# Second attention of a fused transformer kernel: rotary queries from a reordered weight, keys of two heads in one product, squares of the feed-forward residual on ScalarE

## The chip, the cores and the metric

The kernel runs on one core of a Trainium2 chip. One launch computes two transformer blocks for a single sequence of 256 tokens of width 1024, all in 32-bit floats. The metric is the device time of a launch in microseconds (us); the result is compared with the time of the kernel before, measured on the same chip.

## The reference, cut to what matters

The change touches the second half of the first block: the latent attention with shared keys and values (16 heads, handled as 8 pairs), and the norm that follows each of the two feed-forward layers.

```python
def rmsnorm(x, g):
    inv = lax.rsqrt(jnp.mean(x * x, axis=-1, keepdims=True) + RMS_EPS)
    return (x * inv) * g

def rope(x, positions):                  # x: ... x 32
    ang = positions[..., None] * inv_freq    # 16 frequencies
    cos, sin = jnp.cos(ang), jnp.sin(ang)
    x1, x2 = x[..., :16], x[..., 16:]
    return jnp.concatenate([x1 * cos - x2 * sin, x1 * sin + x2 * cos], axis=-1)

def mla_shared_kv(h, ...):
    a = rmsnorm(h, kv_norm) @ w_kv_a                 # 256 + 32 columns
    c_kv = rmsnorm(a[..., :256], ckv_norm)
    k_rope = rope(a[..., 256:][:, :, None, :], positions)   # one for all heads
    k_nope = jnp.einsum('bsr,rhd->bshd', c_kv, w_uk)        # 16 heads x 64
    v = jnp.einsum('bsr,rhd->bshd', c_kv, w_uv)
    return jnp.concatenate([k_nope, broadcast(k_rope)], -1), v

def mla_attention(xn, positions, k, v, ...):
    c_q = rmsnorm(xn @ w_dq, cq_norm)                # 768 wide
    q = (c_q @ w_uq).reshape(B, S, 16, 64 + 32)
    q = jnp.concatenate([q[..., :64], rope(q[..., 64:], positions)], -1)
    o = causal_block_attention(q, k, v, 1 / sqrt(96))
    return o @ w_o

h = h + mla_attention(rmsnorm(h, attn_norm), ...)
h = h + swiglu(rmsnorm(h, ffn_norm), w_gate, w_up, w_down)   # ends both layers
```

## The kernel before, in words

The program is written by hand, engine by engine, in one block for each: `sp` (SyncE) starts the loads, `pe` (TensorE) multiplies, `act` (ScalarE) and `dve` (VectorE) empty PSUM and do the elementwise work. Nothing is reordered by a scheduler: the order of the work on an engine is the order in which its function is written. Engines meet at semaphores. For each of the eight PSUM banks there is `full` (a product is ready) and `free` (it has been read); `take(b)` and `evacuated(b)` on TensorE wait until bank b has been read. Weights come through four buffers `SLOT0` to `SLOT3`: `fill(s, ...)` on SyncE waits until slot s is used up, `here[s]` says that its load has landed, and `release(s)` gives it back when the next product that is passed to `first` completes. Each slot is a single buffer: the next load of a slot starts only after its last product.

Around the change the work runs like this.

1. The first feed-forward layer (`ffn(0)`) ends with its four output tiles (128 tokens x 512 columns each) in banks 0 to 3. `residual` on VectorE adds each to H and squares the sum, with a running sum for the norm. TensorE waits for this.
2. A norm for two users follows. `turned` multiplies H by a diagonal matrix (L533), which scales and turns it in one step, into banks 0 to 3. `gained` (L1769, L1770) reads each bank twice on VectorE, once with the gain of the key norm (into XT2) and once with that of the attention norm (into XT). Ahead of this VectorE clears WPAD, a weight of 96 columns, in which only 64 to 95 are filled (the 32 rope columns of `w_kv_a`, by a load that ScalarE issues). With it the rope part of the keys comes out on partitions 64 to 95.
3. Tables of cosine and sine, the latent keys and queries, and the values follow.
4. Then come the eight head pairs. `mla_proj` computes a pair's queries (12 products, 96 weight columns for each head), then its keys (4 products, 64 columns for each head), and then multiplies the copied queries QRAW by the matrix `rot` (L866, L867), which swaps and negates the rope halves. `rotate` on VectorE makes q x cos + rot(q) x sin in three operations (L2026, L2027, L2029) into QT. `mla_scores` (L874, L875) waits for it. `attend` then turns the probabilities (`flip`, L508), multiplies them by the values (`mix_values`, L502) and turns the output of the pair before.

In the loop over the pairs TensorE does: scores of pair i, projection of pair i+1, attention of pair i. So a projection lies between the scores and the probabilities that come from them, and the pair's own scores come one turn later. Only for pair 0 do the scores follow its projection directly.

At the end of the second feed-forward layer the residual is the same as in the first. After it comes a norm by rows instead of item 2.

## Time and profile before

| | us |
|---|---|
| median of 3 runs | 1939.9 (1938.97 to 1947.72) |
| the profiled execution | 1941.62 |
| its span, first to last instruction | 1939.5 |
| TensorE busy | 1697.2 (88%) |
| VectorE busy | 1054.5 (54%) |
| ScalarE busy | 515.4 (27%) |

The times in the rows are microseconds from the start of the span, then the duration, except where a row says ns. L502 is line 502 of the kernel. Many lines are those of helpers: L502 is every grouped product. A product of 32-bit floats shows as two matmul records, so that 16 products are "x32". PE is TensorE, PEld its weight loads, DVE VectorE, ACT ScalarE, SPq SyncE's queue, ps a PSUM bank. Consecutive matmul records overlap, so the durations of single records don't add up; the times in the chain of waits do. The attention pairs of the change run from 433.8 to about 556 us of the span.

### The profile page before, as it was taken

The numbers are of one execution on the slowest core, as the hardware profiler recorded it, in microseconds if no ns is written. First come the engines' busy times: TensorE is split into PE (matmuls) and PEld (weight loads), VectorE is DVE, ScalarE is ACT, GpSimd is POOL, SyncE is SP. The second block draws the span as 40 slices with busy tenths as digits, with TensorE's granted clock in tenths as the row PEclk, the third lists the DMA queues.
The fourth block names the chain that finished last, engine by engine and source line by source line (L and its number), as shares of the span: only waits on it lengthen the run. The fifth ranks groups of instructions, "written<-read, shape, count | busy, mean of one in ns | idle before, by whom it ended". The sixth has DMA issues, their size and how long they took to land.

```text
span 1939.5 us, 22425 instructions
## 1 busy us (share of the span) xinstructions
PE 1697.2 (88%) x7681; PEld 1178.4 (61%) x7681; DVE 1054.5 (54%) x2463; ACT 515.4 (27%) x1029; POOL 345.8 (18%) x296
## 2 busy tenths in 40 slices
PE   6798999889989998999899999778788878888876
PEld 5787999756649997786565468443333434344332
DVE  5464555533445555255535311477766677766764
ACT  2353444213334442232310001121222222222211
POOL 2550000000000000000000000145344344444440
PEclk9899999999999999999999999989899989889989
DMA  7342665402436654143302415099999999999995
GB/s 240 109 109 88 195 183 177 146 15 60 137 92 184 190 179 140 44 152 131 145 30 88 151 56 196 31 420 420 421 421 421 422 420 421 421 420 422 421 421 240
DMA packets 209719, 435.38 MB, mean 224 GB/s; under 512 B 11649, under 2 KB 145153, under 8 KB 175745
## 3 DMA queue, kind: packets, MB, share of 16 engines
q0 software_dynamic: 36864, 268.45, 33.3%
q1 hardware_dynamic: 171760, 166.06, 27.0%
q8 instruction: 36, 0.59, 0.1%
q10 hardware_dynamic: 1040, 0.13, 0.0%
q14 instruction: 19, 0.15, 0.0%
HBM read 433.53 MB, written 1.05 MB: 224 GB/s over the span
## 4 chain that ended last, share of the span: by engine, by line
PE 68%; DMA 18%; DVE 9%; issue 3%; ACT 1%; POOL 1%; SPq 0%; DVEq 0%; POOLq 0%; ACTq 0%
PE ps L502 37%; DMA OT<-in_peer_uv,IX 16%; PE ps L1297 11%; PE ps L688 6%; PE ps L1002 3%; PE ps L1015 3%; PE ps L533 1%; DMA SLOT<-in_fox_w_in 1%; PE ps L508 1%; DVE SLOT L2422 1%; PE ps L592 1%; DVE SLOT_R L1823 1%; PE ps L1094 1%; PE ps L1212 1%; DVE AR L2137 1%
## 5 line engine op out<-in xcount | busy, mean ns | idle before, releaser
L1706 POOL DMA_INDIRECT SLOT<-in_peer_uv,IX x128 | 134.6, 1052 | 1370.5 <-DVE IX L2416 1123.0
L1297 PE MATMUL ps<-SLOT,AR 128*128 128x512 f32 x512 | 264.6, 673 | 102.5 <-ACT AR L1636 102.5
L1297 PEld LDWEIGHTS ps<-SLOT,AR 128*128 128x128 f32 x512 | 108.5, 217 | 252.2 <-issue 129.6
L502 PE MATMUL ps<-ARH 128*128 128x256 f32 x2112 | 257.0, 283 | 5.2 <-DVE SM L1854 5.2
L502 PEld LDWEIGHTS ps<-ARH 128*128 128x128 f32 x2112 | 256.2, 192 | 7.0 <-issue 5.5
L2422 DVE SCALAR_TENSOR_TENSOR SLOT<-SLOT,V 128x1024 f32<-128x1024 f32 x128 | 153.4, 1225 | 78.9 <-DMA SLOT<-in_peer_uv,IX 76.9
L1823 DVE TENSOR_TENSOR ARH<-SLOT,ARH 128x2048 fp32r<-128x2048 f32 (+1 forms) x88 | 154.1, 1756 | 47.8 <-ACT ARH L1375 31.1
L1297 PE MATMUL ps<-AR 128*128 128x512 f32 x320 | 142.8, 594 | 11.4 <-ACT AR L1636 11.4
L502 PE MATMUL ps<-XT,SLOT 128*128 128x256 f32 x576 | 126.6, 380 | 1.3 <-DVE XT L1770 1.3
L688 PE MATMUL ps<-ARH 128*128 128x512 f32 x528 | 123.9, 390 | 0.0
L502 PEld LDWEIGHTS ps<-XT,SLOT 128*128 128x128 f32 x576 | 108.9, 190 | 16.9 <-issue 1.9
L502 PE MATMUL ps<-SLOT,XT 128*128 128x512 f32 (+3 forms) x320 | 114.6, 517 | 4.0 <-DVE XT L1770 2.6
L1630 ACT ACTIVATE AR<-AR 128x4 f32<-128x4 f32 x64 | 13.1, 205 | 382.7 <-DVE SLOT L2422 182.2
L1297 PEld LDWEIGHTS ps<-AR 128*128 128x128 f32 x320 | 59.7, 190 | 84.0 <-issue 64.3
L688 PEld LDWEIGHTS ps<-ARH 128*128 128x128 f32 x528 | 97.7, 188 | 19.4
L2422 DVE SCALAR_TENSOR_TENSOR AR<-AR,V 128x1024 f32<-128x1024 f32 x80 | 95.3, 1222 | 24.4 <-DMA AR<-in_peer_uv,IX 24.3
L1706 POOL DMA_INDIRECT AR<-in_peer_uv,IX x80 | 90.7, 1134 | 77.2 <-PE ps L1297 72.0
L502 PEld LDWEIGHTS ps<-SLOT,XT 128*128 128x128 f32 x320 | 58.0, 190 | 57.8 <-issue 48.7
L1837 DVE TENSOR_TENSOR AR<-AR,ps 128x256 f32<-128x256 f32 x44 | 18.5, 421 | 125.4 <-ACT AR L1385 125.4
L1636 ACT ACTIVATE AR<-CT,AR 128x128 f32<-128x128 f32 x256 | 81.8, 390 | 17.5 <-DVE AR L2436 17.5
L1375 ACT CAST ARH<-SLOT 128x2048 fp32r<-128x2048 f32 x44 | 83.3, 1897 | 0.0
L502 PE MATMUL ps<-XT 128*128 128x256 f32 (+1 forms) x288 | 60.9, 367 | 7.9 <-DMA XT<-in_w_pq_by_head 5.8
(378 smaller groups left out, 2437.9 us busy)
## 6 DMA issues: line engine op xcount, KB each, us to landing
SLOT<-in_w_gate SPq DMA_DIRECT2D x44, 512.0 KB, 4.0
SLOT<-in_w_up SPq DMA_DIRECT2D x44, 512.0 KB, 5.3
SLOT<-in_w_down SPq DMA_DIRECT2D x44, 512.0 KB, 5.6
SLOT<-in_w_in SPq DMA_DIRECT2D x9, 2048.0 KB, 8.6
SLOT<-in_fox_w_in SPq DMA_DIRECT2D x16, 512.0 KB, 5.3
XT<-in_w_pq_by_head SPq DMA_DIRECT2D x8, 1024.0 KB
SLOT<-in_mla_w_uq SPq DMA_DIRECT2D x8, 576.0 KB
SLOT<-in_fox_w_in SPq DMA_DIRECT2D x2, 2048.0 KB, 13.0
```

Source lines behind the costliest of these rows:

```text
L502: m = pe.matmul(outp, l, r, start=(n_ == 0), stop=(n_ == len(pairs) - 1))
L508: return pe.transpose(outp, src, IDENT)
L533: m = pe.matmul(ps[:, b, n_ * P:(n_ + 1) * P], src[:, n_ % 2, k * P:(k + 1) * P], DG[:, n_ % 2, :], start=True, stop=True)
L688: m = pe.matmul(ps[:, o_, :], l_, r_, start=(start and b == 0 and n_ == 0), stop=(stop and b == 1 and n_ == 2))
L1002: m = pe.matmul(ps[:, b, :], cols(XT, t, k), slot(s_, KC, 512)[:, k, :], start=(k == 0), stop=(k == KC - 1))
L1015: m = pe.matmul(ps[:, b, h * P:(h + 1) * P], l(h), r(h), start=True, stop=True)
L1297: m = pe.matmul(ps[:, 2 * t + c, :], DIAG[:, j, :], v_row(j)[:, c * 512:(c + 1) * 512], start=False, stop=False)
L1375: act.copy(WGU[:, b, 0].rearrange("p g k n -> p (g k n)"), SLOT[b][:, 0:2 * KC * P]).then_inc(sem("high_ready"), 1)
L1636: act.activation(DIAG[:, j, :], IDENT, ACT.Copy, scale=AV[:, t, j:j + 1]).then_inc(sem("diag_ready"), 1)
L1706: pool.indirect_dma_start(PAIR[j], None, pairs, bass.IndirectOffsetOnAxis(IX[:, t, j:j + 1], 0)).then_inc(gathered[j], 16)
L1823: return TT(out_, x, high.bitcast(F32), ALU.subtract)
L2422: m = STT(u_row(j), u_row(j), 1.0, V[:, t, :], ALU.mult, ALU.mult, accum_out=DOT[:, t, j:j + 1])
```

## The change

**Queries.** The host lays out the query weight by pairs in 256 columns instead of 192: for the first head its 64 plain columns, its 32 rope columns, and the same 32 with their halves swapped; for the second head the rope columns, the swapped ones, then the plain ones. The product itself now gives the swapped copy. One table TABQ holds 1 for the plain rows, cosine for the rope rows and signed sine for the swapped ones, and `rotate` is one product of the PSUM bank with it. The rotated keys stand on all 32-row groups, so that the scores' sum over 128 rows adds the cosine and the sine parts. The products with `rot` and the QRAW copy of each pair go; the load of each pair's query weight grows from 576 to 768 KB.

**Keys.** The keys of both heads of a pair are one group of 2 products with 128 columns instead of two groups of 2 with 64. ScalarE copies the result in two pieces of 64 partitions by 256 instead of one of 64 by 512.

**Key rope.** WPAD becomes a loaded weight of 128 columns (`w_krope`, the 32 columns four times, 512 KB) in the upper half of SLOT3. The clearing, the signal and ScalarE's load go. TensorE waits for `here[3]` twice 16 ahead of this product instead of ahead of the values.

**The norm for two users.** VectorE writes only XT2; ScalarE writes XT from the same banks after it. TensorE starts when XT2 is whole (`norm_low`), and waits for banks 2 and 3 later.

**Squares.** At the end of both feed-forward layers VectorE only adds and signals (`grown`), and ScalarE squares with a running sum; VectorE waits for `squared`.

```diff
-            fill(3, (slot(3, 2, D), w_uv))
-            qk(rows(w_uq, 0, 192), w_uk[:, :, 0:P])
+            fill(3, (WPAD, rows(a["w_krope"], 0, P)), (slot(3, 2, D), w_uv))
+            qk(rows(w_uq, 0, 2 * P), w_uk[:, :, 0:P])
             with T.loop("mla", PAIRS - 1) as i:
-                qk(dyn(w_uq, i * 192 + 192, 192), w_uk[:, :, ds(i * P + P, P)])
+                qk(dyn(w_uq, i * 2 * P + 2 * P, 2 * P), w_uk[:, :, ds(i * P + P, P)])
...
-            norm_t()
-            pe.wait_ge(sem("wpad_here"), T.next(sem("wpad_here"), 17))
+            turned(H, KC, freer="a")
+            pe.wait_ge(here[3], T.next(here[3], 32))
+            pe.wait_ge(sem("norm_low"), T.next(sem("norm_low"), 4))
             take(4)
-            group(ps[0:96, 4, 0:S], ((WPAD[:, k, :], XT2[:, k, :]) for k in range(KC))).then_inc(full["a"][4], 1)
+            group(ps[:, 4, 0:S], ((WPAD[:, k, :], XT2[:, k, :]) for k in range(KC))).then_inc(full["a"][4], 1)
             T.add(free["a"][4])
...
             pe.wait_ge(here[2], T.next(here[2], 16))
+            evacuated(2, 3)
...
-                    m = group(ps[0:96, 0, hh * S:(hh + 1) * S], ((slot(0, 6, 192)[:, k, 96 * hh:96 * hh + 96], CQT[:, k, :]) for k in range(6)))
+                    m = group(ps[:, 0, hh * S:(hh + 1) * S], ((slot(0, 6, 2 * P)[:, k, P * hh:P * hh + P], CQT[:, k, :]) for k in range(6)))
                 release(0)
-                m.then_inc(full["a"][0], 1)
-                T.add(free["a"][0])
+                m.then_inc(full["v"][0], 1)
+                T.add(free["v"][0])
                 pe.wait_ge(here[1], T.next(here[1], 16))
                 take(6)
-                for hh in range(2):
-                    m = group(ps[0:64, 6, hh * S:(hh + 1) * S], ((slot(1, 2, P)[:, k, 64 * hh:64 * hh + 64], CKT[:, k, :]) for k in range(2)))
+                group(ps[:, 6, 0:S], ((slot(1, 2, P)[:, k, :], CKT[:, k, :]) for k in range(2))).then_inc(full["a"][6], 1)
                 release(1)
-                m.then_inc(full["a"][6], 1)
                 T.add(free["a"][6])
-                take(7)
-                evacuated(0)
-                first(pe.matmul(ps[0:96, 7, 0:S], const("rot", 96), QRAW[0:96, 0, :], start=True, stop=True))
-                pe.matmul(ps[0:96, 7, S:2 * S], const("rot", 96), QRAW[0:96, 1, :], start=True, stop=True).then_inc(full["v"][7], 1)
-                T.add(free["v"][7])
 
             def mla_scores(i):
-                evacuated(6, 7)
+                evacuated(0, 6)
                 for hh in range(2):
...
+                for c in range(2):
+                    for t in range(NT):
+                        act.wait_ge(sem("grown"), T.next(sem("grown")))
+                        m = act.activation(XS[:, t, c * 512:(c + 1) * 512], H[:, t, c * 512:(c + 1) * 512], ACT.Square,
+                                           accum_out=SS[:, 10 + NT * c + t:11 + NT * c + t])
+                m.then_inc(sem("squared"), 1)
...
-            act.wait_ge(sem("wpad_here"), 1)
-            act.dma_start(WPAD[:, :, 64:96], rows(a["w_kv_a"], 256, 288)).then_inc(sem("wpad_here"), 16)
+            for g in range(4):
+                act.wait_ge(sem("norm_low"), T.next(sem("norm_low")))
+                for k in (2 * g, 2 * g + 1):
+                    m = act.activation(XT[:, k, :], ps[:, g, k % 2 * S:k % 2 * S + S], ACT.Copy, scale=gcol("attn1", k, 1))
+                m.then_inc(free["a"][g], 1)
             act.wait_ge(sem("angle_ready"), T.next(sem("angle_ready")))
-            act.activation(COS[0:96, 0, :], ANG[0:96, 0, :], ACT.Sin)
-            act.activation(SIN[0:96, 0, :], ANG[0:96, 1, :], ACT.Sin).then_inc(sem("sin_ready"), 1)
+            act.activation(COS, ANG[:, 0, :], ACT.Sin)
...
             def mla_copy():
-                act.wait_ge(full["a"][0], T.next(full["a"][0]))
-                act.copy(QRAW[0:96, :, :], view(ps[0:96, 0, :], 2, S)).then_inc(free["a"][0], 1)
                 act.wait_ge(full["a"][6], T.next(full["a"][6]))
-                act.copy(KT[0:64, :, :], view(ps[0:64, 6, :], 2, S)).then_inc(free["a"][6], 1)
+                act.copy(KT[0:64, 0, :], ps[0:64, 6, 0:S])
+                act.copy(KT[64:P, 1, :], ps[64:P, 6, 0:S]).then_inc(free["a"][6], 1)
 
...
+            def ffn_residual():
+
+                for c in range(2):
+                    for t in range(NT):
+                        b = 2 * t + c
+                        dve.wait_ge(full["v"][b], T.next(full["v"][b]))
+                        half = H[:, t, c * 512:(c + 1) * 512]
+                        TT(half, half, ps[:, b, :], ALU.add).then_inc(free["v"][b], 1)
+                        T.add(free["v"][b])
+                        settled(b)
+                        signal("grown")
+                dve.wait_ge(sem("squared"), T.next(sem("squared")))
...
-            dve.memset(WPAD[:], 0.0).then_inc(chain, 1)
+            scaled(H, D, squared=True).then_inc(sem("xs_ready"), 1)
+            for g in range(4):
+                dve.wait_ge(full["v"][g], T.next(full["v"][g]))
+                TT(XT2[:, 2 * g:2 * g + 2, :], view(ps[:, g, :], 2, S), inner(gcol("kv", 2 * g, 2), S), ALU.mult).then_inc(sem("norm_low"), 1)
...
-            signal("wpad_here")
-            norm("attn1", X2=XT2, name2="kv")
...
-            dve.tensor_copy(COS[R96, 1, :], COS[R96, 0, :])
-            dve.tensor_copy(SIN[R96, 1, :], SIN[R96, 0, :]).then_inc(chain, 1)
+            dve.memset(TABQ[0:64, 0, :], 1.0)
+            dve.memset(TABQ[64:P, 1, :], 1.0)
+            dve.tensor_copy(TABQ[64:96, 0, :], COS[64:96])
+            dve.tensor_copy(TABQ[0:32, 1, :], COS[0:32])
+            TS(TABQ[96:P, 0, :], SIN[96:P], const("sign")[96:P], None, ALU.mult)
+            TS(TABQ[32:64, 1, :], SIN[32:64], const("sign")[32:64], None, ALU.mult).then_inc(chain, 1)
...
-            dve.tensor_copy(KT[64:96, 0, :], KRT[64:96, :])
-            dve.tensor_copy(KT[64:96, 1, :], KRT[64:96, :]).then_inc(chain, 1)
+            dve.tensor_copy(KT[64:P, 0, :], KRT[64:P, :])
+            dve.tensor_copy(KT[0:64, 1, :], KRT[0:64, :]).then_inc(chain, 1)
...
             def rotate():
-                dve.wait_ge(full["v"][7], T.next(full["v"][7]))
-                TT(ANG[R96, 0:2, :], view(ps[R96, 7, :], 2, S), SIN[R96, :, :], ALU.mult)
-                TT(ANG[R96, 2:4, :], QRAW[R96, :, :], COS[R96, :, :], ALU.mult).then_inc(chain, 1)
-                dve.wait_ge(chain, T.next(chain))
-                TT(QT[R96, :, :], ANG[R96, 0:2, :], ANG[R96, 2:4, :], ALU.add).then_inc(free["v"][7], 1)
-                T.add(free["v"][7])
+                dve.wait_ge(full["v"][0], T.next(full["v"][0]))
+                TT(QT[:], view(ps[:, 0, :], 2, S), TABQ, ALU.mult).then_inc(free["v"][0], 1)
+                T.add(free["v"][0])
...
+    arrays["in_w_krope"] = np.ascontiguousarray(np.tile(np.asarray(inputs["w_kv_a"])[:, KVR:], (1, P // ROPE)))
+    uq = np.asarray(inputs["mla_w_uq"])[0].reshape(QR, PAIRS, 2, NOPE + ROPE)
+    nope, rope = uq[..., :NOPE], uq[..., NOPE:]
+    swapped = np.concatenate([rope[..., ROPE // 2:], rope[..., :ROPE // 2]], 3)
+    by_pair = [nope[:, :, 0], rope[:, :, 0], swapped[:, :, 0], rope[:, :, 1], swapped[:, :, 1], nope[:, :, 1]]
+    arrays["in_w_uq_by_pair"] = np.ascontiguousarray(np.concatenate(by_pair, 2).reshape(QR, PAIRS * 2 * P))
```

Engine TensorE, one turn of the pair loop, from the last part of the scores to the turning of the first head's probabilities; before:

```order
L875 MATMUL ps<-AR 128x256
L850 ISA
L502 MATMUL ps<-AR,SLOT 96x256 [waits free_a0,free_v0,slot_here0]
L502 MATMUL ps<-AR,SLOT 96x256 x11
L857 REGISTER_ALU
L502 MATMUL ps<-AR,SLOT 64x256 [waits free_a6,free_v6,slot_here1]
L502 MATMUL ps<-AR,SLOT 64x256 x3
L485 REGISTER_ALU [waits free_v0,free_a7,free_v7]
L866 MATMUL ps<-AR,CT 96x256 [waits free_a0]
L867 MATMUL ps<-AR,CT 96x256
L622 ISA
L508 MATMUL ps<-CT,AR 128x128 [waits free_a3,free_v3,probs_ready]
```

and after:

```order
L871 MATMUL ps<-AR 128x256
L853 ISA
L504 MATMUL ps<-AR,SLOT 128x256 [waits free_a0,free_v0,slot_here0]
L504 MATMUL ps<-AR,SLOT 128x256 x11
L860 REGISTER_ALU
L504 MATMUL ps<-AR,SLOT 128x256 [waits free_a6,free_v6,slot_here1]
L504 MATMUL ps<-AR,SLOT 128x256
L624 ISA
L487 REGISTER_ALU [waits free_v3,probs_ready]
L510 MATMUL ps<-CT,AR 128x128 [waits free_a3]
```

Two of the four key products and both products with `rot` (ps<-AR,CT) are gone, and with the latter the wait for bank 0 inside the projection.

Engine VectorE, the same turn of the loop, from the second head's maxima to the reciprocal of the sums; before:

```order
L1801 TENSOR_REDUCE SM<-AR 128x1 [waits free_v2]
L1801 TENSOR_REDUCE SM<-AR 128x1
L2025 REGISTER_ALU
L2026 TENSOR_TENSOR AR<-ps,AR 96x512 [waits full_v7]
L2027 TENSOR_TENSOR AR<-AR 96x512
L2028 ISA
L2029 TENSOR_TENSOR AR<-AR 96x512 [waits dve_chain]
L1808 REGISTER_ALU
L1808 REGISTER_ALU [waits probs_ready]
L1809 RECIPROCAL SM<-SM 128x8 [waits probs_ready]
```

and after:

```order
L1818 TENSOR_REDUCE SM<-AR 128x1 [waits free_v2]
L1818 TENSOR_REDUCE SM<-AR 128x1
L2045 REGISTER_ALU
L2046 TENSOR_TENSOR AR<-ps,AR 128x512 [waits full_v0]
L1825 ISA
L1825 REGISTER_ALU [waits probs_ready]
L1826 RECIPROCAL SM<-SM 128x8 [waits probs_ready]
```

One operation on the query bank itself (full_v0) stands where three waited for the `rot` bank (full_v7).

Engine ScalarE, end of the first feed-forward layer and the norm for two users; before:

```order
L1385 ACTIVATE AR<-ps 128x256 [waits full_a5]
L1340 ACT_TABLE_LOAD
L1340 ACTIVATE RS<-RS 128x2 [waits rms_ready]
L1453 DMA AR<-in_w_kv_a 128x8x32 [waits wpad_here]
L1455 ACT_TABLE_LOAD
L1455 ACTIVATE AR<-AR 96x256 [waits angle_ready]
```

and after:

```order
L1381 ACTIVATE AR<-ps 128x256 [waits full_a5]
L1409 ACTIVATE XS,SS<-H 128x512 [waits grown] x4
L1336 ACT_TABLE_LOAD
L1336 ACTIVATE RS<-RS 128x2 [waits rms_ready]
L1457 ACTIVATE XT<-ps,GCOL 128x256 [waits norm_low]
L1457 ACTIVATE XT<-ps,GCOL 128x256
```

The four squares (L1409) stand between the last gate activation and the table load for the square root, and the writes of XT stand ahead of the sine.

## Rows read from the trace of the kernel before

**Rows 1.** The page: shares of the span in the chain of waits.

```profile
PE 68%; DMA 18%; DVE 9%; issue 3%; ACT 1%; POOL 1%; SPq 0%; DVEq 0%; POOLq 0%; ACTq 0%
```

**Rows 2.** Chain of waits, one turn of the loop: start, us, what, records.

```profile
470.75 0.46 PE ps L874 x2
...
472.30 7.05 PE ps L502 x32
479.36 0.60 PE ps L866 x2
...
480.75 0.49 ACT AR L1361
...
481.71 0.88 PE ps L502 x6
...
483.54 0.46 PE ps L874 x2
```

**Rows 3.** Chain of waits, the first two projections, before the loop.

```profile
433.78 7.26 PE ps L502 x32
...
444.33 0.46 PE ps L874 x2
...
446.70 7.91 PE ps L502 x32
454.61 0.60 PE ps L866 x2
...
456.59 1.52 PE ps L502 x12
```

**Rows 4.** One line: ScalarE copies of 64 partitions by 256, ns min/median/max.

```profile
L1429 ACT COPY AR<-ps x8: 365/365/366, 68.9 to 138.5; 64x256 f32<-64x256 f32 x8
```

**Rows 5.** Timeline of SyncE's queue: a query load's issue in the loop.

```profile
491.06 0.37 SPq L351 DMA_DIRECT2D SLOT<-in_mla_w_uq  x1
```

**Rows 6.** Windows: busy us by engine, granted clock, DMA share, GB/s.

```profile
494.00:494.50 0.50, 0.00 (x0) 0.00 (x0) 0.49 (x1) 0.40 (x2) 0.00 (x0) 1.00 1.08 369
495.00:495.50 0.50, 0.50 (x7) 0.50 (x7) 0.33 (x2) 0.00 (x0) 0.00 (x0) 1.00 0.24 69
...
521.00:522.00 1.00, 0.85 (x9) 0.73 (x7) 0.04 (x1) 0.37 (x1) 0.00 (x0) 1.00 0.64 92
...
446.00:447.00 1.00, 1.00 (x4) 0.64 (x3) 0.95 (x5) 0.23 (x1) 0.00 (x0) 0.50 0.00 0
```

**Rows 7.** Timeline, end of the first feed-forward layer: start, us, engine, line.

```profile
364.96 5.63 PE L688 MATMUL ps<-ARH 128*128 128x512 f32 x24
368.59 0.69 DVE L1791 TENSOR_TENSOR H<-H,ps 128x512 f32<-128x512 f32 x1 [1.80 <-PE ps L688]
...
374.26 0.70 DVE L1965 MEMSET AR<- 128x768 f32 x1 [0.23 <-DVE XS L1794]
375.00 0.15 DVE L1736 COPY SM<-SM 128x1 f32<-128x1 f32 x1
...
375.66 0.20 ACT L1340 ACTIVATE RS<-RS 128x2 f32<-128x2 f32 x1 [8.81 <-DVE RS L1728]
```

**Rows 8.** Timeline, the norm for two users.

```profile
376.43 5.55 PE L533 MATMUL ps<-AR,H 128*128 128x128 f32 x32 [5.84 <-DVE AR L1753]
...
383.23 0.68 DVE L1770 TENSOR_TENSOR XT<-ps,GCOL 128x512 f32<-128x512 f32 x1
...
384.48 3.67 PE L502 MATMUL ps<-XT,AR 128*96 128x256 f32 x16 [2.50 <-DVE XT L1770]
```

**Rows 9.** Timelines: square root after the second feed-forward layer; an exposed table load.

```profile
770.33 0.20 ACT L1340 ACTIVATE RS<-RS 128x2 f32<-128x2 f32 x1 [7.83 <-DVE RS L1728]
...
810.13 1.28 ACT L1503 ACT_TABLE_LOAD   x1
811.42 0.94 ACT L1503 ACTIVATE AR<-AR 128x384 f32<-128x384 f32 x2
```

**Rows 10.** Groups by shape: a ScalarE activation of 128x512, busy us, mean ns.

```profile
L1528 ACT ACTIVATE XS<-ps 128x512 f32<-128x512 f32 x4 | 2.4, 602 | 1.8 <-PE ps L1002 1.8
```

More of the change, by code:

```diff
@@ L48 @@
                ("half0", 128), ("half1", 128), ("dmask", 128), ("causal", 256), ("sb_neg", 384), ("sb_keep", 384),
[L49 removed]
+               ("lev", 6 * 128), ("levT", 6 * 128), ("rot", 128), ("inv_freq", 1), ("sign", 1), ("iota16", 16), ("zero", 128)]:
     _COLS[_n] = (_at, _w)
@@ L79, in constant_table @@
     put("levT", np.concatenate([a.T for a in lev], 1))
-    rot = np.zeros((96, 96))
-    for r in range(ROPE // 2):
-        rot[NOPE + 16 + r, NOPE + r] = -1.0
-        rot[NOPE + r, NOPE + 16 + r] = 1.0
+    rot = np.zeros((P, P))
+    for b in range(0, P, ROPE):
+        for r in range(ROPE // 2):
+            rot[b + 16 + r, b + r] = -1.0
+            rot[b + r, b + 16 + r] = 1.0
     put("rot", rot)
     inv = np.float32(10000.0) ** (-np.arange(ROPE // 2, dtype=np.float32) * np.float32(2.0) / np.float32(ROPE))
-    put("inv_freq", np.concatenate([np.zeros(NOPE), inv, inv])[:, None])
+    put("inv_freq", np.tile(inv, P // 16)[:, None])
+    put("sign", np.where(np.arange(P) % ROPE < ROPE // 2, -1.0, 1.0)[:, None])
     put("iota16", np.repeat(np.arange(16)[None], P, 0))
@@ L208, in program @@
         CUMT = arena(8928, S, parts=16)
-        QRAW = arena(9056, 2, S)
-        COS = arena(9568, 2, S)
-        SIN = arena(10080, 2, S)
-        WPAD = arena(10592, KC, 96)
+        TABQ = arena(9056, 2, S)
+        COS = arena(9568, S)
+        SIN = arena(10080, S)
+        WPAD = view(SLOT[3][:, 2 * D:2 * D + KC * P], KC, P)
         KVA = arena(11360, NT, 768)
@@ L523, in transposes, with turned @@
                     T.add(free["v"][b])
-            def turned(src, n_chunks, banks=(0, 1, 2, 3), reader="v"):
+            def turned(src, n_chunks, banks=(0, 1, 2, 3), reader="v", freer="v"):
                 pe.wait_ge(sem("xs_ready"), T.next(sem("xs_ready")))
@@ L536, in turned @@
                     m.then_inc(full[reader][b], 1)
-                    T.add(free["v"][b])
+                    T.add(free[freer][b])
             def norm_t(reader="v"):
@@ L833, in _ @@
             take(5)
-            pe.matmul(ps[0:96, 5, 0:S], const("rot", 96), KRT[0:96, :], start=True, stop=True).then_inc(full["v"][5], 1)
+            pe.matmul(ps[:, 5, 0:S], const("rot"), KRT, start=True, stop=True).then_inc(full["v"][5], 1)
             T.add(free["v"][5])
@@ L837, in _ @@
             evacuated(0)
-            pe.wait_ge(here[3], T.next(here[3], 16))
             for c in range(2):
@@ L1450, in _ @@
             root()
-            act.wait_ge(sem("wpad_here"), 1)
-            act.dma_start(WPAD[:, :, 64:96], rows(a["w_kv_a"], 256, 288)).then_inc(sem("wpad_here"), 16)
+            for g in range(4):
[3 more added lines that the diff above has]
+                m.then_inc(free["a"][g], 1)
             act.wait_ge(sem("angle_ready"), T.next(sem("angle_ready")))
-            act.activation(COS[0:96, 0, :], ANG[0:96, 0, :], ACT.Sin)
-            act.activation(SIN[0:96, 0, :], ANG[0:96, 1, :], ACT.Sin).then_inc(sem("sin_ready"), 1)
+            act.activation(COS, ANG[:, 0, :], ACT.Sin)
+            act.activation(SIN, ANG[:, 1, :], ACT.Sin).then_inc(sem("sin_ready"), 1)
             act.wait_ge(full["a"][4], T.next(full["a"][4]))
-            act.copy(KRT[0:96, :], ps[0:96, 4, 0:S]).then_inc(free["a"][4], 1)
+            act.copy(KRT, ps[:, 4, 0:S]).then_inc(free["a"][4], 1)
             for t in range(NT):
```

45 lines of the change are left out of this document (21 added, 24 removed).

## The prediction

> **What bounds the kernel now.** I read the chain of waits on the page first. Over the whole span it lies 68% on TensorE [rows 1]. The weight loads and gathers of its 18% are not touched. So I went to the stretches that the change names and read there, in order of time, what TensorE waits for. The chain in the pair loop shows a turn of 12.8 us (470.75 to 483.54) in which TensorE hardly stops: scores 1.55, projection 7.05, the `rot` products, and one stop, for ScalarE's copy of the turned probabilities and then until 481.71 [rows 2]. Every TensorE product that goes there shortens the kernel, unless that one stop grows. Ahead of the loop the chain shows the only place where scores wait for their own projection: keys done at 441.04, scores at 444.33 [rows 3]. The timelines of the feed-forward end and the norm show TensorE standing still while VectorE adds, squares, clears and scales [rows 7, 8]. So three kinds of places count: TensorE's own work, the wait of pair 0, and VectorE's chains around the norms.
>
> **The pair loop, six turns.** The projection is 32 records in 7.05 us, 0.220 each, in one piece though 24 of them carry 96 weight columns and 8 carry 64 [rows 2]. The keys go from 8 records to 4: 4 x 0.220 = 0.88 us less. From the end of the keys to the first product with the values it is now 479.36 to 481.71 = 2.35 us [rows 2]: `rot`, a flip, a copy of 0.49 on ScalarE, and 0.47 of issue. Without `rot` the flip is early, and ScalarE comes last: two key copies of 0.365 [rows 4], with 0.02 to start 0.75, then the 0.49 and the 0.47, together 1.71. So 0.64 goes there and not the whole of `rot`: the split key copy is late next. A turn loses 1.52 us; six turns 9.1 us. VectorE has one operation instead of three and is waited for by nobody there; the QRAW copy was under the key products.
>
> **The second projection,** written out ahead of the loop: keys end 454.61, values begin 456.59, 1.98 us [rows 3]. Without the register work of a loop the issue is some 0.3, so 0.75 + 0.49 + 0.3 = 1.54. With the key products 0.44 + 0.88 = 1.3 us.
>
> **Pair 0.** Queries multiplied by the table are one VectorE operation of about 0.7 us (the 128x512 product from PSUM takes 0.68 [rows 8]), and it starts 0.88 before the keys end, so it is done before ScalarE's key copies. Scores then start 0.75 + about 0.15 for two more waits after the keys: 0.9, against 444.33 - 441.04 = 3.29. With 0.88 of key products: 3.3 us.
>
> **The clock after it.** At 446 to 447 us the granted clock is 0.50 [rows 6], the 1.2 GHz level: these scores take 2.37 us (444.33 to 446.70) [rows 3] where the loop has 1.55 [rows 2], and the projection behind them 7.91 instead of 7.05 [rows 3]. That is 1.7 us, which came after TensorE had stood for over 2 us. With a stop of 0.9 I expect no fall: 1.7 us. Both ends for the range: 0 and 1.7. The Trainium skill (TensorE: Matmul & The Clock Gate, on the clock gate) says that the gate's monitor runs free and does not start with the kernel, so where it falls may differ between runs of one kernel; one trace can't show that, and by this rule the term could as well be lost or come up at another stop.
>
> **End of the first feed-forward layer.** The 24 records from 364.96 to 370.6 fill the four banks 0.7 us apart [rows 7]. Now VectorE adds and squares from 368.59 to about 374.05, clears WPAD in 0.70, signals in 0.15, and the square root starts at 375.66 [rows 7]. After: four times an add of 0.69 and a signal of 0.15 with about 0.5 of waiting for the second bank makes 368.59 + 3.4 + 0.5 = 372.5; the last square on ScalarE, a 128x512 activation of 0.60 [rows 10], ends at 373.1. But the square root needs its table. Now that load is done while ScalarE idles; after, it stands behind the last square: 1.28, and the next activation follows in 0.01 [rows 9], so the root starts at 374.5. VectorE's two short steps in between are hidden under it. 1.1 us less (1.8 without the load). TensorE's first product follows as far behind the root as now.
>
> The Trainium skill (ScalarE: Activation LUTs, What ACT_TABLE_LOAD costs) adds a drain of about 1.38 us to each switch, 2.66 in all. The row has 1.28 + 0.01 and no drain; by the page the sum below would be 2.8 us smaller.
>
> **End of the second feed-forward layer.** The same steps 395.65 later put the root at 770.15 against 770.33 now [rows 9], as no clearing goes there: 0.1 us, nothing but the swap of VectorE's squares for an exposed table load.
>
> **The norm for two users.** TensorE turns from 376.43 for 5.55 us [rows 8]; VectorE ends at 383.91 and the first product comes at 384.48, 8.05 after the start. With four reads instead of eight VectorE keeps up with the banks: last bank at 5.55, one read of 0.68, and 0.2 for fewer waits behind it: 6.4. 1.6 us less. ScalarE's writes of XT come 0.9 later and are needed only by the third product group, over 7 us on; the sine, the tables and TABQ (six short operations instead of two) lie under the products of the latent projections.
>
> **Loads.** `w_krope` adds 512 KB to slot 3, which is empty before the layer's last products begin at 364.96 [rows 7]; the product that needs it comes at about 382. Even with the 4 MB of the other projections' weights around it, 4.5 MB at 369 GB/s [rows 6] are 13 us of those 17, and most of them are under way earlier, so I cost it at nothing; without that cover it would be late by up to 1.4. The query load is the tight one. It is issued at 491.06 [rows 5], 6.86 before the next projection (472.30 plus two turns, 497.9). After, this distance is 6.86 - 0.88 - 0.64 = 5.3. Now the traffic of both loads ends by about 495.2, 4.1 after the issue, at up to 369 GB/s [rows 6]. The added 192 KB take 0.5: 4.7, hidden with 0.6 to spare. If the cover goes, each 0.1 us costs 0.7 over the seven pairs.
>
> **The sum.** 9.1 + 1.3 + 3.3 + 1.7 + 1.1 + 0.1 + 1.6 = 18.2 us, about half of it in the loop. The profiled execution took 1941.6 (span 1939.5), so it becomes 1923.4. The median of the runs shown, 1939.9, is 1.7 below it; for a median I forecast 1939.9 - 18.2 = 1921.7 us. Everything after the second feed-forward layer should only move earlier.
>
> **Rivals.**
> - The clock falls at pair 0 anyway, or at another stop: 1923.4. For it: the fall shown came after the products had begun again. Against: TensorE hardly stops now.
> - ScalarE drains around the exposed table load for about as long again as the load of 1.28 [rows 9]: twice 1.3 lost, 1924.3. The page cited above stands for it. Against: 0.01 between load and activation in the row.
> - The query load shows. Landing at 6 us instead of 4.7 costs 0.7 x 7 = 4.9 us: 1926.6; at 7 us, 12: 1933.6. For it: 0.6 to spare only. Against: the rate is far from any limit.
> - 128 weight columns cost more than 96, that is, the change adds TensorE work where it says it only fills it: a third more on 24 records is 1.76 us a pair, 14 us on eight: 1935.8. Against: 96 and 64 columns run at one pace [rows 2].
> - Slower than before: the query load, in one single buffer, runs at the rate of a crowded moment, 92 GB/s [rows 6]. Both loads of a pair are 896 KB then, 10 us, with 1 us of start 11 after the issue, 5.7 late on seven pairs: 40 us, 1961.7. It decides from a landing 7.9 us after the issue (2.6 x 7 = 18.2). Place: the start of each projection. Against: the row lies where the output weights load at the same time, and there it lasts 1 us.
>
> **How the numbers follow.** Forecast 0.73, clock 0.10, drain 0.03, load shown 0.08, columns 0.03, slower 0.03. Half a per cent, 9.7 us, is about what a measurement can tell here. Forecast, clock, drain and five of the eight hundredths of the load case are below 1930.2: faster 0.91. The rest of it and the columns are within: 0.06. Slower 0.03. The low end: the turning after the first layer runs its first part at half clock now; if that falls away up to 1.9 us more go, with the clock of later stretches and the measurement 1917. The high end takes in clock, drain and a stall of 0.5 a pair, 1928.5.
>
> **What would show it.** In the loop: turns of about 11.3 us, 28 records in about 6.2 us, no line with `rot` and two copies of 64x256 between the keys and the copy of the probabilities; that copy should start 0.75 after the keys. Pair 0: scores within 1 us of its keys, and the granted clock at 1.0 there. After the feed-forward layers: a table load directly behind the fourth square and in front of the root, at both places. The first product of the key rope 6.4 us after the turning starts. Wrong: TensorE waiting for a DMA at the queries; a gap of over 0.1 us between table load and root when VectorE is done; a projection of 7 us; or a gain under 12 us with all these in place, which would mean that later stages give time back.

## The result, and the profile after the change

The changed kernel takes 1930.03 us (median; 1926.3 to 1933.57, 8 runs), the kernel before on the same chip 1940.61 (1938.13 to 1947.72, 8 runs): a ratio of 0.9943, 95% interval 0.9927 to 0.9959. So the gain is clear of the noise, but it is 10.6 us, not 18.2. The time lies outside the range that was given, above it. The profiled execution took 1930.27 us, with a span of 1928.1 and a mean granted clock of 0.951, against 0.955 in the one before.

The chain of waits of the changed kernel, as the page gives its shares (the answer to [rows 1]):

```profile
PE 67%; DMA 18%; DVE 8%; issue 3%; ACT 2%; POOL 1%; SPq 0%; DVEq 0%; POOLq 0%; ACTq 0%
```

Nothing changed sides: TensorE sets the end as before. So the answer has to be read stretch by stretch. First one turn of the loop, from the chain of waits of the changed kernel (start, us, what, records), the answer to [rows 2]:

```profile
467.16 6.06 PE ps L504 x28
...
473.62 0.32 ACT AR L1481
474.01 0.49 ACT AR L1357
...
474.86 0.88 PE ps L504 x6
...
476.58 0.46 PE ps L870 x2
...
478.13 6.06 PE ps L504 x28
```

A turn is 10.97 us instead of 12.8. It holds 28 records in 6.06; the next thing is the second key copy on ScalarE, then the copy of the turned probabilities, which starts 0.79 after the keys. This is the picture that was forecast, with a gain of 1.8 instead of 1.52.

The two stretches where it went otherwise stand ahead of the loop. The same view, from the values' group of 16 to the third projection (the answer to [rows 3]):

```profile
414.82 8.85 PE ps L504 x16
...
427.34 5.49 PE ps L535 x24
...
433.98 5.87 PE ps L504 x26
440.05 4.88 DMA SLOT<-in_w_uq_by_pair
444.96 5.89 PE ps L504 x26
451.07 4.76 DMA SLOT<-in_w_uq_by_pair
455.87 6.33 PE ps L504 x28
```

Two things are to be seen. A DMA now stands in the chain ahead of the second and third projection. And in front of the first projection the products for the values take 8.85 and the turning of the queries 5.49. The kernel before has the same products, of the same size, in this view:

```profile
418.86 7.15 PE ps L502 x16
...
429.69 2.94 PE ps L533 x24
```

These are 1.7 and 2.55 us less than now, for unchanged work. The windows of the changed kernel say why (columns as in [rows 6]; the clock is the number behind the engines):

```profile
417.00:418.00 1.00, 1.00 (x3) 0.34 (x2) 0.61 (x1) 0.00 (x0) 0.00 (x0) 0.50 0.00 0
428.00:429.00 1.00, 1.00 (x7) 1.00 (x7) 0.00 (x0) 0.00 (x0) 0.00 (x0) 0.50 0.00 0
...
446.00:447.00 1.00, 1.00 (x6) 0.89 (x5) 0.00 (x0) 0.00 (x0) 0.00 (x0) 1.00 0.00 0
```

At 446 us, where [rows 6] has 0.50, the clock is now 1.00, as forecast. But it is at 0.50, the 1.2 GHz level, in the two stretches before.

The end of the first feed-forward layer, ScalarE's part of the changed kernel's timeline (the answer to [rows 7]):

```profile
370.18 0.63 ACT L1409 ACTIVATE XS<-H 128x512 f32<-128x512 f32 x1
...
370.92 1.28 ACT L1336 ACT_TABLE_LOAD   x1
372.21 0.20 ACT L1336 ACTIVATE RS<-RS 128x2 f32<-128x2 f32 x1
```

The table load stands directly behind the fourth square, and the root 0.01 behind it. In the chain of waits it is 10.11 us from the start of the layer's last products to the turning (362.88 to 372.99), 11.31 before (365.12 to 376.43). The norm for two users, from the timeline (the answer to [rows 8]):

```profile
372.99 6.49 PE L535 MATMUL ps<-AR,H 128*128 128x128 f32 x32 [4.64 <-DVE AR L1757]
...
379.51 0.69 DVE L1985 TENSOR_TENSOR XT<-ps,GCOL 128x512 f32<-128x512 f32 x1 [0.31 <-PE ps L535]
...
380.30 0.89 PE L504 MATMUL ps<-XT,SLOT 128*128 128x256 f32 x3 [0.83 <-issue]
```

VectorE now waits for TensorE's banks and not the reverse. The first product starts 7.31 behind the turning (6.4 forecast, 8.05 before), because the turning itself takes 6.49 instead of 5.55: the clock is low for more of it.

### The profile page after: what moved, and what is told of

Same layout as the page of the kernel before. It is cut to its first block, busy times and chain, and to the rows that moved or that the text cites. A ratio compares the mean times of both kernels' runs of the same rounds, so it can differ in the third digit from the quotient of the medians.

```text
span 1928.1 us, 22250 instructions
## 1 busy us (share of the span) xinstructions
PE 1690.2 (88%) x7617; PEld 1181.8 (61%) x7617; DVE 1039.2 (54%) x2437; ACT 521.2 (27%) x1053; POOL 343.3 (18%) x296
## 4 chain that ended last, share of the span: by engine, by line
PE 67%; DMA 18%; DVE 8%; issue 3%; ACT 2%; POOL 1%; SPq 0%; DVEq 0%; POOLq 0%; ACTq 0%
PE ps L504 37%; DMA OT<-in_peer_uv,IX 16%; PE ps L1293 11%; PE ps L690 6%; PE ps L998 3%; PE ps L1011 3%; PE ps L535 1%; DMA SLOT<-in_fox_w_in 1%; PE ps L510 1%; DVE SLOT L2439 1%; PE ps L594 1%; DVE SLOT_R L1840 1%; PE ps L1090 1%; PE ps L1208 1%; DVE AR L2154 1%
## 5 line engine op out<-in xcount | busy, mean ns | idle before, releaser
L1293 PE MATMUL ps<-SLOT,AR 128*128 128x512 f32 x512 | 269.9, 684 | 96.5 <-ACT AR L1640 96.5
L1293 PE MATMUL ps<-AR 128*128 128x512 f32 x320 | 143.5, 597 | 10.5 <-ACT AR L1640 10.5
L504 PEld LDWEIGHTS ps<-XT,SLOT 128*128 128x128 f32 x592 | 111.8, 190 | 18.2 <-issue 2.9
## 6 DMA issues: line engine op xcount, KB each, us to landing
SLOT<-in_fox_w_in SPq DMA_DIRECT2D x2, 2048.0 KB, 13.2
```

Of the source, the lines that this page charges most:

```text
L504: m = pe.matmul(outp, l, r, start=(n_ == 0), stop=(n_ == len(pairs) - 1))
L1293: m = pe.matmul(ps[:, 2 * t + c, :], DIAG[:, j, :], v_row(j)[:, c * 512:(c + 1) * 512], start=False, stop=False)
```

## The experiments

Two theories stood after this. The clock theory: the parts of the change do what they should, and the granted clock, low at the values and the queries' turning, takes several us back. The load theory: the query weight, which has one single buffer, lands late. A simple edit takes away either.

To take the clock out of a comparison I use filling: in a stop, TensorE multiplies the identity by a constant into an idle bank, and nothing reads it. In the diffs of this section `warm` is this function:

```
+def warm(n, b=4, w=512):
+    take(b)
+    for _ in range(n):
+        first(pe.matmul(ps[:, b, 0:w], IDENT, CT[:, 0:w], start=True, stop=True))
```

### Query weight loaded early, alone (early_q)

```
 qk(rows(w_uq, 0, 2 * P), w_uk[:, :, 0:P])
-with T.loop("mla", PAIRS - 1) as i:
+fill(2, (slot(2, 6, 2 * P), rows(w_uq, 2 * P, 4 * P)))
+fill(1, (slot(1, 2, P), w_uk[:, :, P:2 * P]))
+with T.loop("mla", PAIRS - 2) as i:
```

Pair 1's query weight goes into slot 2, which is free at that time, and `mla_proj(2)` reads it there. The other loads stay as they were.

> The changed kernel with one edit: the query weight of pair 1 is loaded into slot 2 ahead of time, so that the second projection doesn't wait for a load that starts only when the first has used slot 0 up. Theory of the late load: TensorE's waits for the query load (439.97 to 444.92 of the profile, about 2.6 us after the scores, and 0.3 at 455.8) go, 2.9 us less than the changed kernel, about 1927. Rival, the load is only where an unavoidable wait shows: no change, 1930.

Measured: 1931.36 us (1926.36 to 1936.36, 6 runs), ratio 0.9945 (0.9928 to 0.9962): no difference from the changed kernel. Its chain of waits:

```profile
434.15 6.30 PE ps L506 x28
...
443.12 6.04 PE ps L506 x28
...
453.44 6.06 PE ps L506 x28
```

The DMA is gone from this part of the chain, and from the first to the third projection it takes 19.3 us instead of 21.9. The times don't show these 2.6 us; they are at the rival's 1930 and not at the theory's 1927. The six executions lie 10 us apart, with mean clocks of 0.947 to 0.954, so this run alone settles nothing.

### Filling in every stop, after and before (awake, before_awake)

```
+warm(2)                         # ffn: ahead of the turning, and behind it
+warm((4, 11)[l], 7)             # ffn: behind the last block
...
+warm(2, 4, 256)                 # ahead of the products for the values
+warm(3, 7)                      # ahead of the queries' turning
...
+warm(1, 7, 256)                 # ahead of pair 0's scores (before: 4 in bank 5)
+warm(4, 7, 256)                 # changed kernel only: behind them, at the DMA
...
+warm(1, warm_bank, 256)         # attend: ahead of the products with the values
...
+warm(1, 4, 256)                 # last pair: ahead of the turning of its output
+warm(1, 4, 128)                 # and behind it
```

> The changed kernel with products that nothing reads put into TensorE's stops (ends of both feed-forward layers, norms, ahead of the values' and queries' products, in each turn of the pair loop), each shorter than the stop. Theory of the clock: the stretches at granted clock 0.50 at 373 to 379, 416 to 420, 427 to 433, 487 to 490, 511 to 514 and 765 to 771 us go, some 12 us less, about 1918. Rival, the stretches at half clock cost nothing because VectorE or ScalarE ends last there, or the products delay the work: 1928 to 1932.

> The kernel before with the same filling products in the same stops. Theory of the clock: before has half clock at 376 to 380, 445 to 449, 551 to 555 and 777 to 783 us, some 8 us: about 1933. The distance from it to the changed kernel with filling products is then the change without the clock: 13 to 15 us, and with the early load 16 to 18 us, the forecast's sum without its clock term. Rival, the forecast's durations were too large by themselves: the distance stays at 10 to 11 us, as between the two kernels without filling.

Measured: the changed kernel with filling 1921.08 us (1915.73 to 1922.57, 5 runs), ratio 0.9875 (0.9856 to 0.9895). The kernel before with filling 1938.05 (1935.37 to 1941.68, 12 runs), ratio 0.9971 (0.9962 to 0.9981). Both have a mean clock of 0.959 in the profiled execution. Filling gives 4.9 us to the kernel before (by the ratio 5.6), where some 8 were expected. To the changed kernel it gives 9.0 by the medians; its unfilled runs were timed in another batch, in which the kernel before was 2.4 us faster, and by the ratios (0.9943 and 0.9875) it is 13.2. The chain of `awake`:

```profile
413.84 7.15 PE ps L510 x16
...
424.67 2.94 PE ps L541 x24
...
434.88 4.81 DMA SLOT<-in_w_uq_by_pair
439.73 5.89 PE ps L510 x26
```

Values and turning are back at 7.15 and 2.94; the DMA is still there. Between the two filled kernels lie 17.0 us, between the unfilled ones 10.6. So the clock theory holds: the clock takes more from the changed kernel, 4.0 us by what filling gave in the medians, 6.4 by these two distances, 7.6 by the ratios. The intervals of the four ratios are wide enough to leave a doubt; the next run takes it away.

### Both (early_q_awake)

The two edits together, without the four products at the DMA, as no DMA is waited for there any more.

> Both edits at once. If both theories hold the gains add: about 1915. If the late load only used time that the clock would take anyway: as the kernel with the filling products alone.

Measured: 1916.28 us (1915.87 to 1918.42, 4 runs), ratio 0.9864 (0.9845 to 0.9883). It beats both kernels: it is 26.7 us below the one before (1942.98 in the same batch) and 13.8 below the changed one. Against `awake` it is 4.8 less, against `before_awake` 21.8, where 16 to 18 were expected (the traces have 18.9 of it in the stretch that the change touches). And it is 15.1 us below `early_q`, which differs from it by the filling alone and was timed in the same batch. By the ends of the two intervals that is 9 to 23 us, where filling gives the kernel before 3.7 to 7.4. This is the comparison which shows clear of the noise that the clock takes more from a kernel with the change. Its chain at pair 0:

```profile
427.06 6.30 PE ps L512 x28
...
434.52 0.46 PE ps L885 x2
...
436.07 6.04 PE ps L512 x28
...
446.38 6.06 PE ps L512 x28
```

Pair 0 is now what the prediction described: scores 1.16 behind the keys (0.9 forecast), with nothing in between but the two key copies on ScalarE (0.36 and 0.38) and 0.39 of issue. From the first to the second projection it is 9.01, in `awake` 10.92, in `before_awake` 12.09; to the third 10.31, 11.01 and 11.92. The traces give 2.6 us to the early load here too. The rest of the distance of the two spans (1919.5 and 1914.1) lies almost all where nothing differs: 1.7 ahead of the first layer's last products, 0.9 behind the second layer. So the trace shows 2.6 for the early load, and the 4.8 of the medians holds something of one execution against the next.

### The keys of two heads at once, without the rope columns (keys_only_awake)

```
-    for hh in range(2):
-        m = group(ps[0:64, 6, hh*S:(hh+1)*S], (... 64 weight columns))
+    group(ps[:, 6, 0:S], (... 128 weight columns))
...
+    act.copy(KT[0:64, 0, :], ps[0:64, 6, 0:S])
+    act.copy(KT[0:64, 1, :], ps[64:P, 6, 0:S])
```

`before_awake` with this alone; `rot`, the QRAW copy and the tables stay as they were.

> The kernel before with the filling products, and only the keys of the change: one group of 2 products with 128 columns for both heads, two ScalarE copies. The products with rot stay. Theory: 0.88 us a pair less and nothing more, since the longer copy (0.75 instead of 0.58) lies under the rot products: 7 us less than the kernel before with filling products, 1931. Rival, the copy is late: 0 to 5 us less.

Measured: 1929.45 us (1925.09 to 1932.07, 6 runs), ratio 0.9919 (0.9897 to 0.9942): 8.6 less than `before_awake` (10.1 by the ratios). A turn in its chain of waits:

```profile
464.97 6.04 PE ps L508 x28
...
476.68 6.05 PE ps L508 x28
```

and in the one of `before_awake`:

```profile
468.26 7.05 PE ps L508 x32
...
481.09 4.10 PE ps L508 x19
```

The projection goes from 7.05 to 6.04, and the turn from 12.83 to 11.71. Four records less are worth 1.01, not the 0.88 of 4 x 0.220, so the gain is above the 7 us that were expected. The late copies don't show here: they lie beside the products with `rot`. The turn of the whole change is 11.0, so the rope columns give the other 0.7.

### The squares back on VectorE (squares_back_awake)

```
-for each block: act.activation(XS[...], H[...], ACT.Square, accum_out=...)
-ffn_residual()
+residual(lambda c, t: 2 * t + c)
```

`early_q_awake` with this edit alone.

> The changed kernel with the early load and the filling products, but the squares after the feed-forward layers on VectorE again. Theory of the exposed table load: from the first add to the square root 6.1 us instead of 5.87 at the first layer and 6.1 instead of 5.9 at the second, so 0.2 to 0.3 a layer: 0.5 us more in all, which the times can hardly tell. Rival, the squares on ScalarE are worth their own 0.7 us a tile on VectorE's chain: 1.5 a layer, 3 us more.

Measured: 1917.74 us (1915.57 to 1918.66, 5 runs), ratio 0.986 (0.9836 to 0.9884), against 1916.28 and 0.9864 of `early_q_awake`: no difference in the times. The chain of waits:

```profile
373.01 0.71 DVE XS L1823 x2
...
374.35 0.21 ACT RS L1354
...
375.12 3.84 PE ps L543 x32
```

From the last products to the turning it is 10.32 us here, 10.10 in `early_q_awake`; behind the second layer 15.94 against 15.74. So the squares on ScalarE are worth 0.2 us a layer. Of the 1.2 us at the first layer's end 1.0 comes from the clearing of WPAD and its signal (11.31 in `before_awake`, 10.32 here), which this kernel does not have either: `w_krope` arrives complete. The square on VectorE is 0.7 behind each add; the one on ScalarE stands beside the adds, but pays with 1.28 of table load in front of the root.

### VectorE writes both outputs of the norm again (norm_back_awake)

```
-for g in range(4): ACT copies XT, DVE writes XT2
+norm("attn1", X2=XT2, name2="kv")
```

`early_q_awake` with this edit alone.

> The changed kernel with the early load and the filling products, but VectorE writes both XT2 and XT again, eight reads instead of four, and TensorE waits for all four banks. Theory: with the clock high the turning takes 3.84 us and VectorE with eight reads of 0.6 is last: 2 to 2.4 us more. Rival: no difference, because ScalarE's writes hold the banks as long.

Measured: 1919.97 us (1916.72 to 1921.25, 5 runs), ratio 0.9875 (0.9851 to 0.9899). The chain of waits:

```profile
374.36 0.69 DVE XT L1785
375.05 0.60 DVE XT L1786
...
378.63 0.61 DVE XT L1786
...
379.81 1.32 PE ps L512 x5
```

VectorE's eight reads are the chain. From turning to key product it is 6.65 us, in `early_q_awake` 4.67: 1.98 at this place. In the times it is 3.7 by the medians and 2.1 by the ratios, with intervals that overlap; they go along with the 1.98.

### Filling at three places only (fill_three)

```
+warm(4, 7)         # ahead of the turning of the first norm
+warm(2, 4, 256)    # ahead of the products for the values
+warm(3, 7)         # ahead of the queries' turning
```

On the changed kernel, late load and all.

> The changed kernel, filled only in the three stops between the first feed-forward layer and the first pair where all profiles of changed kernels without filling had the clock low: ahead of the turning, of the values, and of the queries' turning. Theory: the turning goes from 6.2 to 6.5 us to 3.85, the values from 8.85 to 7.15, the queries' turning from 5.5 to 2.94, 6.5 us less together: about 1924. Rival, the low clock only moves on to the next stop, the pair loop: 1927 to 1930.

Measured: 1926.74 us (1919.68 to 1930.28, 6 runs), ratio 0.9922 (0.9907 to 0.9937). The profiled execution is the shortest of the six (span 1917.6, clock 0.959); its chain:

```profile
411.37 7.15 PE ps L510 x16
...
422.20 2.94 PE ps L541 x24
...
432.37 4.77 DMA SLOT<-in_w_uq_by_pair
```

In this execution the three places are at full pace, and the low clock does not move on to the pair loop (66.1 us from the third projection to the output projection, as in `awake`). In the times it is worth 3.3 us by the medians and 4.1 by the ratios: the median of 1926.74 is nearer to the rival's 1927 than to the theory's 1924. What the longer executions lost, and where, isn't in a trace. So the sum of the three places by the chain (1.7 and 2.55, and 2.4 to 2.6 from the norm's turning to its key product) is only partly seen in the times.

### The same kernels once more (after_again, after_again2, before_again, before_again2)

No edit: three traces of each kernel tell what belongs to the kernel and what to one execution.

> The changed kernel once more, unaltered, for a second profile. Theory that the clock's falls move from one execution to the next: the stretches of 31.2 us of key and query products and the pair loop's turns of 10.97 us stand, but the granted clock is 0.50 at other stops than in the first profile, where it was 371 to 379, 416 to 420, 426 to 433, 487 to 490 and 511 to 514 us. Rival, the falls are fixed by the kernel's own stops: the same five places.

> The kernel before once more, unaltered, for a second profile. If the clock's falls in the norm stretches are the changed kernel's own, values and queries' turning stay at 7.15 and 2.94 us here; if they differ from one execution to the next, one of them shows 8.85 or 5.5.

> A third profile of the kernel before, with the same two expectations as the second.

> A third profile of the changed kernel: if the falls are its own, turning, values and queries' turning at 6.2 to 6.5, 8.85 and 5.5 us again; if they differ from one execution to the next, at least one at full clock.

Measured: the changed kernel 1932.49 and 1928.48 us, where the medians of the kernel before on those chips were 1945.05 and 1942.04; the kernel before 1944.64 and 1951.57. Those two single differences are 12.6 and 13.6. The chain of the last one, `after_again2`:

```profile
416.25 8.84 PE ps L504 x16
...
428.77 5.49 PE ps L535 x24
```

and the longest one of the kernel before, `before_again2`:

```profile
431.94 5.40 PE ps L533 x24
```

The last products of the output projection, in `before` and in `after`:

```profile
551.01 5.21 PE ps L599 x8
```

```profile
540.22 3.67 PE ps L601 x8
```

In the table a row with "to" runs from the start of the one to the start of the other; the others are durations in the chain of waits.

| us | before, 3 traces | after, 3 traces | before_awake | early_q_awake |
|---|---|---|---|---|
| last products to turning | 11.3, 11.3, 11.3 | 10.1, 10.1, 10.1 | 11.31 | 10.10 |
| turning to key product | 8.1, 8.1, 8.1 | 7.3, 7.1, 7.1 | 6.65 | 4.67 |
| products for the values | 7.15 (all) | 8.85, 8.85, 8.84 | 7.15 | 7.15 |
| queries' turning | 2.94, 2.94, 5.40 | 5.49 (all) | 2.94 | 2.94 |
| first to second projection | 12.9, 12.8, 12.1 | 11.0, 11.2, 11.0 | 12.09 | 9.01 |
| second to third | 12.8, 12.9, 13.6 | 10.9, 12.6, 10.9 | 11.92 | 10.31 |
| third to output projection | 76.6, 76.6, 76.6 | 69.4, 66.0, 66.1 | 76.86 | 65.80 |
| last products of the output projection | 5.21, 5.30, 5.37 | 3.67, 5.37, 3.67 | 3.67 | 3.67 |
| turning behind the second layer | 6.74, 6.78, 6.76 | 6.55, 5.29, 5.34 | 3.85 | 3.85 |
| first layer's last products to that turning | 411.6, 411.7, 418.6 | 402.5, 401.2, 397.7 | 407.3 | 388.4 |

The fall at the values is in every trace of the changed kernel and in none of the one before. The one at the last products of the output projection is in every trace before and in one of three after, so there the clock gives 1.6 us to the change. In the loop a fall is in one of three traces of the changed kernel (487 to 514 us of the first, 3.4 us), and the second projection's in one of three. So some falls belong to the kernel and some to the execution.

The last row takes in all that the change touches. `awake` has 391.2 there, `fill_three` 390.9 and `early_q` 395.2. Against the filled kernel of its own kind each trace before has 4.3, 4.4 and 11.3 us more, each trace after 11.3, 10.0 and 6.5. So in the middle ones the clock costs the changed kernel 5.6 more, but one pair of executions can have it the other way round. Ahead of that row, where the engines do the same work in both kernels, the chain reaches the first layer's last products at 365.1, 368.1 and 367.4 before and at 362.9, 362.8 and 364.6 after. These differences of half a us to 5 us are in the distance of the whole executions too, and the traces name no cause for them.

## Why the prediction was right in most of its parts and wrong in its sum

Point by point, by the prediction's own steps. The first column of numbers is the forecast, the second what `early_q_awake` against `before_awake` shows, where neither clock nor load is in the way.

| step | forecast | shown |
|---|---|---|
| loop, six turns | 9.1 | 11.06 |
| second projection | 1.3 | 1.61 |
| pair 0 | 3.3 | 3.08 |
| end of the first layer | 1.1 | 1.21 |
| end of the second layer | 0.1 | 0.22 |
| norm for two users | 1.6 | 1.98 |
| sum without the clock | 16.5 | 19.2 |

Small losses at other places (from the key product to the values 0.15, from the output projection to the second layer's last products 0.15) and gains (0.05) leave 18.9 over the whole stretch from the first layer's last products to the turning behind the second.

- **The pair loop: right, and a little low.** The mechanism is the one named, TensorE's records and then ScalarE's split key copy. The term was mis-sized in three places: the projection gives 1.01 a turn and not 0.88; from the keys' end to the values it is 1.64 and not 1.71; and from the values to the next scores it is 1.72, where [rows 2] has 1.83. Filling costs the kernel before some 0.3 us in these turns (76.86 against 76.6), so without it the loop gains 10.5.
- **Pair 0 and the second projection: right as work, but hidden by the load.** This is the first step that failed, in the words of the prediction: "After, this distance is 6.86 - 0.88 - 0.64 = 5.3", and "0.6 to spare", for all seven pairs. For the last five of them this is nearly what the trace shows: issue at 473.00, next projection at 478.13, 5.1 us, with no wait. The landing is right as well: 4.88 and 4.76 against 4.7. But the distance of pair 1 is another. Before, it ran from the issue behind pair 0's query products over the keys, the long stop and the slow scores to the second projection at 446.70, 6.7 us:

```profile
439.96 0.38 SPq L351 DMA_DIRECT2D SLOT<-in_mla_w_uq  x1
```

  The prediction itself took 3.3 and 0.8 us out of that stretch and did not carry them over to the load. Its own numbers leave 2.6 there, against a landing of 4.7: a wait of 2.1. The timeline of the changed kernel shows what is left:

```profile
440.05 0.38 SPq L353 DMA_DIRECT2D SLOT<-in_w_uq_by_pair  x1
...
442.39 0.60 PE L871 MATMUL ps<-AR 128*128 128x256 f32 x2
...
444.96 1.35 PE L504 MATMUL ps<-AR,SLOT 128*128 128x256 f32 x5 [1.98 <-DMA SLOT<-in_w_uq_by_pair]
```

  The scores end 2.9 us behind the issue, the data land 4.9 behind it, and TensorE waits 1.98. At pair 2 it waits 0.32 more. Together 2.3 us (2.5 and 2.3 in the two later traces), for which the sum had nothing. TensorE waiting for a DMA at the queries is what the prediction had named as a sign of being wrong, but it had priced it only as one stall for all pairs.
- **The clock after pair 0: the term 1.7 failed, by its sign.** The fall at pair 0 is gone, as said. But in its place the clock is low at the values and at the queries' turning, 1.7 and 2.55 us, and the first norm's turning gets slower. The prediction took its clock term from pair 0 alone, where the trace of before had a fall. It named another stop as a rival, but gave no price to the stops that stay as long as they were: 411.99 to 414.82 after, 416.14 to 418.86 before. By the filled kernels the clock costs 9.0 us after and 4.9 before (by the ratios 13.2 and 5.6): a loss of 4.0 to 7.6 where a gain of 1.7 stood. The Trainium skill (TensorE: Matmul & The Clock Gate, the part on the clock gate) says that the monitor runs free, so that the point where the clock changes may differ between runs. The traces agree in the loop, one of three; at the values they show no such difference, three of three after and none of three before. Why the stop at the values costs the clock in the one kernel and not in the other isn't settled. The only thing that the runs show is that it goes when the stops are filled.
- **The end of the layers: right.** 1.2 us, against 1.1. The load of the table is exposed as forecast. The squares have next to no part in it: `squares_back_awake` gives them 0.2, and the clearing 1.0. The forecast had said as much for the second layer, where nothing is cleared. The Trainium skill (ScalarE: Activation LUTs, What ACT_TABLE_LOAD costs) adds a drain of about 1.38 us. The row has the load at 370.92 for 1.28 and the root at 372.21, so no drain is in it, and the measurement decides.
- **The norm for two users: right, and hidden in part by the clock.** 1.98 with the clock high, 0.7 to 1.0 with the clock as it was granted.
- **The columns: right.** 128 weight columns run at the pace of 96: 28 records in 6.04 to 6.06.

- **The range.** Its high end was to take in the clock, the drain and 0.5 us on seven pairs. These are 1.7, 2.6 and 3.5, and make 1929.5 and not 1928.5; the measured 1930.03 lies above either.

The bill: 18.9 us of work, less 2.3 for the load that shows, less 4.0 to 7.6 for the clock makes 9.0 to 12.6. The clock's part has the least certain size. The first comparison has 10.6, its interval reaches from 8.0 to 14.2 (0.9959 and 0.9927 of 1940.6), and the two later executions, one each, have 12.6 and 13.6.

Two rivals had part of it. "The clock falls at another stop" had 0.10 and gave 1923.4, too small, since it took back only its own 1.7. "The query load shows" had 0.08, and was worked out as one stall for all pairs. That both could come together with a clock that costs more than before was not among the cases. The argument against the second, "the rate is far from any limit", isn't in the rows either: the one with 369 GB/s has the DMA engines' share at 1.08. The landing came at 4.7 to 5.1 all the same; it was the distance that was short.

## What to carry to other kernels

When a change takes a stop out of TensorE's path, subtract that stop from the distance of every transfer that was issued before it and is waited for behind it, pair by pair and not only for the steady turn of the loop: 3.3 us saved at pair 0 were paid back with 2.0 at its next load. A stop of TensorE costs more than its own length where the clock falls; look at the granted clock at all stops, not just at the one that goes, and try filling them with products that nothing reads: here the filling of every stop was worth 9 to 15 us of 1930 in the kernels with the change, and 5 in the one before. And a part that moves work off VectorE may be worth little when it puts a table load on the chain in its place: 0.2 us a layer here.

## What was not expected of the hardware

- The clock differs between two kernels at the same stop: the 16 products for the values take 7.15 us in three of three traces before and 8.84 to 8.85 in three of three after, behind stops of 2.7 and 2.8 us.
- Four of 32 records of a projection taken away give 1.01 us (7.05 to 6.04), 0.25 each, though the mean over the 32 is 0.220. Eight records with 64 weight columns, in two groups, had become four with 128 in one.
- A load of the query weight takes 4.67 to 5.06 us from issue to landing wherever it stands in the chain, in the traces of the changed kernel, filled or not.
- From the turning behind the second layer to the end the six traces of the two kernels have 1162.7 us (`after`, `before_again`) to 1166.4 (`after_again`). No edit reaches there, so these 3.7 us belong to the execution, and they are more than most parts of this change are worth.
